# Page gathers of the sample's attention issued ahead, and the planner told of it

## Chip, cores and metric

The kernel runs on one core of a Trainium2 chip. The metric is the device time of one execution in microseconds (us). TensorE (PE) multiplies matrices, VectorE (DVE) and ScalarE (ACT) do elementwise work, GpSimd (POOL) does nothing here but issue indirect DMAs (gathers), and SyncE (SP) issues all the other DMAs. Each engine takes its own instructions strictly in order and waits on semaphores for the others.

## What is computed

One decoder layer is applied to a prompt of 1024 tokens and to a sample batch of 8 sequences of 4 new tokens, each sequence with 2048 cached tokens in pages of 128. After an input projection there are two mixers, a sparse attention and a retention; behind them stands a product-key expert layer (PEER) that gathers 128 expert rows for each token.

```python
# sparse attention of the sample batch
sc = indexer_scores(qi, wi, all_ik)          # all_ik: index keys by page, and the new ones
_, sel = lax.top_k(sc, 256)
k_sel = cache_k_l[phys, off]; v_sel = cache_v_l[phys, off]
att = sparse_attend(qa, k_sel, v_sel, valid)
...
# expert layer, for each token: 8 heads x 16 experts
hval = jnp.einsum('thkd,td->thk', u_emb[eid], xb)
coef = gate * gelu(hval)
y = jnp.einsum('thk,thkd->td', coef, v_emb[eid])
```

## The kernel before

Tokens are worked in nine tiles: tiles 0 to 7 are 128 prompt tokens each, tile 8 holds the 32 sample tokens. Each tile passes a front (attention and retention), a back (output projection, norm, choice of the experts) and its experts. The experts are the bulk. One slot is one expert of each of the tile's 128 tokens: an indirect DMA fetches 128 rows of 2048 floats (1.05 MB) into one of the 8 buffers of `ring`; VectorE forms the dot product of its first half with the tokens (L1476); ScalarE makes a 128x128 diagonal of coefficients from it; TensorE adds diagonal times second half to `yacc` (L1023). Two slots make a unit. In the order of work `unit` is the gather, the dot product and the diagonal, and `sums` the products on TensorE. There are 528 units in all, numbered 0 to 527 here: tile 6 has units 384 to 447. The gather of a slot waits until the slot eight before it has been summed (`row_used`), so at most four units are gathered ahead of `sums`.

A planner, `make_schedule`, writes one list of steps before the kernel is built, and every engine issues its part of each step in the order of that list. It keeps a clock for TensorE and one for VectorE, gives each step a cost and a lag (the time from its end to when the next step of its stream may start), and takes, among the steps that could start soonest, the one that is due first. So a lag in a table like `front_steps` decides how many units stand between two steps, on every engine.

The front of tile 8 computes the sample's attention beside the experts of tiles 5, 6 and 7:

- `sspread`, `swi`, `swiT` lay out the index weights; then nine steps `sscores`. Step b below 8 turns index-key page b on TensorE (L1094), ScalarE copies it, TensorE adds the weighted scores of page b-1 (L1102) and forms the dots of page b (L1108). Step 8 ends the sum. The sum goes by four small DMAs of SyncE to another place (`spare<-mid`), and `splace` (L1555) copies it together on VectorE.
- 32 steps `topk` on VectorE (MAX8 on L1338, MATCH_REPLACE8 on L1339) pick 256 of 2080 scores; `slogits` steps stand between them. Step (b, c) turns a quarter of key page b (L1135, bank `sKT`) and forms logits. After `mask`, the softmax and four steps `svalue` with the value pages; then key pages 4 to 7 and value pages 4 to 7 for the second half of the sequences.
- Beside them run the steps of the back of tile 7: `out` (L960, with chunks of `w_out` that SyncE loads two ahead), `add`, `norm`, `peerq`, `keys`, `top`.

The page gathers, 8 of index keys (0.52 MB each), 8 of keys and 8 of values (1.05 MB each), are issued by GpSimd between the expert gathers, from one place:

```python
pool.indirect_dma_start(dst, None, table, bass.IndirectOffsetOnAxis(ap=ids, axis=0)).then_inc(s, 16)
```

They land in two halves of `G` (the front of `kv`), in a part of `Hb`, and in a part of `spare`. Each is issued at the step that uses it, with a wait on the step that read the buffer before.

Of the kernel before, what the change touches and what calls it, by code (L numbers as in the profile page):

```python
# [24 lines left out]
P = 128  # L25
D = 1024
# [201 lines left out]
def front_steps(t):  # L228
# [27 lines left out]
    else:  # L256
        steps = [Step("load", t, 0, "", 0, 1, 12.0), Step("sheads", t, 0, "P", 3.0, 1, 2.5), Step("spad", t, 0, "D", 4.0, 2, 0.3),
                 Step("sdecay", t, 0, "P", 1.2, 2), Step("sdecayed", t, 0, "D", 4.5, 1, 0.3), Step("sret", t, 0, "P", 10.0, 1, 0.5)]
        for k in range(NB + 1):
            if k < NB:  # L260
                steps += [Step("skd", t, k, "D", 0.6, 0, 0.3), Step("sstate", t, k, "P", 1.7, 1, 0.4)]
            if k:
# [4 lines left out]
                  Step("swiT", t, 0, "D", 1.6, 1, 0.3)]  # L267
        steps += [Step("sscores", t, b, "P", 6.5, 1, 8.0 if b < NB else 1.2) for b in range(NB + 1)]
# [6 lines left out]
        for g in range(2):  # L275
            if g:
                steps += [Step("slogits", t, (b, c), "P", 2.0, 1, 1.2 if c < 5 else 4.0) for b in range(4, 8) for c in range(6)]
# [68 lines left out]
def make_schedule():  # L346
# [19 lines left out]
    def arrival(t, k):  # L366
        free = chosen[t] + LATENCY
# [104 lines left out]
def build(nc, x_p, x_s, cache_k, cache_v, cache_ik, state_in, pages, w_in, w_out, w_q, sk, uv,  # L472
# [15 lines left out]
    with ExitStack() as ctx:  # L488
# [66 lines left out]
        gathered = [G, Hb[:, 768:2816]]  # L555
        gathered_v = [G, spare[:, 2048:4096]]
# [120 lines left out]
        g_used = sem("g_used")  # L677
        smax_ready = sem("smax_ready")
# [137 lines left out]
        def _(pe):  # L816
# [268 lines left out]
            def sscores(t, b_):  # L1085


                if b_ < NB:
                    pe.wait_ge(g_in[b_ % 2], 16 * (b_ // 2 + 1))
                    for half in range(2):  # L1090
                        b = claim(("skT", b_, half))
                        for j in range(4):
                            c = 1024 * (b_ % 2) + (4 * half + j) * P
                            mm = nc.tensor.transpose(b[:, j * P:(j + 1) * P], G[:, c:c + P], ident)  # L1094
                        fill(mm, ("skT", b_, half))
# [29 lines left out]
            def slogits(t, part):  # L1125
# [3 lines left out]
                pe.wait_ge(g_in[bb % 2], 16 * (4 + 4 * g + bb // 2 + 1))  # L1129
# [42 lines left out]
            def svalue(t, part):  # L1172
# [4 lines left out]
                pe.wait_ge(g_in[bb % 2], 16 * (4 + 4 * g + 2 + bb // 2 + 1))  # L1177
# [639 lines left out]
        def _(pool):  # L1817
# [18 lines left out]

            def sscores(t, b):
                if b == NB:
                    return
                if b == 0:  # L1840
                    pool.wait_ge(gi_ready, 1)
                    pool.wait_ge(states_out, 16)
                if b >= 2:
                    filled(pool, ("skT", b - 2, 1))
                gather(G[:, 1024 * (b % 2):1024 * (b % 2 + 1)], table_ik, gi[:, b:b + 1], g_in[b % 2])

            def slogits(t, part):
# [78 lines left out]
```

## Time and profile before

| | us |
|---|---|
| median of 3 runs | 3803.05 (3802.86 to 3806.05) |
| the profiled execution, its own time | 3804.14 |
| its span in the trace | 3802.3 |
| VectorE busy in the span | 2595.7 |
| TensorE busy in the span | 3148.6 |

The span is the part of the execution that the trace shows; about 2 us lie around it. The page cuts it into 40 slices of 95 us, and gives busy shares in tenths; the DMA row there is the mean of the core's 16 DMA engines.

### The profile page before, as it was taken

Reading aid. Unit: us, or ns where it says so; the run is one execution under the profiler, and the core shown is the slowest. Engines: PE = TensorE matmul, PEld = TensorE weight load, DVE = VectorE, ACT = ScalarE, POOL = GpSimd, SP = SyncE. Lnnn points to the kernel's source line nnn. Section 1 sums busy time; section 2 is a strip of 40 time slices with the busy share of each in tenths; the row PEclk is TensorE's granted clock in tenths of the full one; section 3 lists DMA queues with packets and bytes.
Section 4 is the critical chain, followed back from the end, with each engine's and each line's share of the span. In section 5 each row is a group of like instructions: output and inputs, shape, how many; then the busy total and the mean of one; then the engine's idle time right before and its main releaser. Section 6 shows DMA issues by size and latency. Waiting matters only on the chain.

```text
span 3802.3 us, 31960 instructions
## 1 busy us (share of the span) xinstructions
PE 3148.6 (83%) x9551; PEld 1542.0 (41%) x9551; DVE 2595.7 (68%) x6051; ACT 1250.8 (33%) x3568; POOL 1240.7 (33%) x1084
## 2 busy tenths in 40 slices
PE   5999855898789879987987899789888288896877
PEld 2444344443244435433543454345433144342421
DVE  1222137877877878898889888998855998443645
ACT  1111122263235424532542264226333033331322
POOL 0000001444334434442443344334342034442432
PEclk9999977999999989998998999899999589998999
DMA  4111132999999999998999999899998179997998
GB/s 173 53 53 51 44 148 104 420 420 421 369 421 410 421 362 407 421 420 360 411 416 366 363 398 417 339 371 409 358 400 353 54 291 421 421 384 268 421 421 344
DMA packets 190430, 1245.76 MB, mean 328 GB/s; under 512 B 22704, under 2 KB 27184, under 8 KB 50672
## 3 DMA queue, kind: packets, MB, share of 16 engines
q0 software_dynamic: 155520, 1128.34, 72.8%
q1 hardware_dynamic: 34736, 115.37, 8.0%
q8 instruction: 77, 1.26, 0.1%
q14 instruction: 97, 0.79, 0.1%
HBM read 1220.50 MB, written 22.46 MB: 327 GB/s over the span
## 4 chain that ended last, share of the span: by engine, by line
PE 47%; DMA 25%; DVE 21%; issue 2%; ACT 2%; SPq 1%; POOL 1%; ACTq 0%; DVEq 0%; POOLq 0%
PE yacc L1023 24%; DMA weights<-in_uv,eid 20%; PE bank L850 11%; DVE weights L1476 6%; DVE kv L1339 4%; DVE tiny L1338 3%; PE bank L986 3%; PE bank L960 2%; DMA weights<-in_w_out 2%; DMA out_y_p<-nw 1%; PE bank L936 1%; PE bank L914 1%; DVE weights L1208 1%; POOL weights L1823 1%; SPq L715 1%
## 5 line engine op out<-in xcount | busy, mean ns | idle before, releaser
L1023 PE MATMUL yacc<-weights,diag 128*128 128x512 f32 (+1 forms) x4224 | 1961.0, 613 | 234.9 <-ACT diag L1743 234.3
L1823 POOL DMA_INDIRECT weights<-in_uv,eid x1056 | 1212.8, 1148 | 2503.5 <-PE yacc L1023 1797.1
L1476 DVE CUSTOM_DVE_ANT_0 weights<-weights,xn 128x1024 f32<-128x1024 f32 x1056 | 1274.8, 1225 | 598.0 <-DMA weights<-in_uv,eid 584.8
L1023 PEld LDWEIGHTS yacc<-weights,diag 128*128 128x128 f32 (+1 forms) x4224 | 791.4, 193 | 1295.4 <-issue 901.6
L1733 ACT ACTIVATE gl<-hv 128x2 f32<-128x2 f32 x528 | 107.1, 203 | 1522.2 <-DVE hv L1476 1521.2
L1743 ACT ACTIVATE diag<-main,coef 128x128 f32<-128x128 f32 x1024 | 359.0, 394 | 156.6 <-PE yacc L1023 140.7
L1736 ACT ACTIVATE coef<-gl,gate 128x1 f32<-128x1 f32 x1056 | 253.4, 287 | 17.3
L960 PE MATMUL bank<-weights 128*128 128x512 f32 (+1 forms) x288 | 160.9, 697 | 109.4 <-DMA weights<-in_w_out 107.6
L1338 DVE MAX8 tiny<-kv 128x8 f32<-128x384 f32 (+6 forms) x224 | 245.0, 1094 | 3.1
L1339 DVE MATCH_REPLACE8 kv<-tiny,kv 128x384 f32<-128x384 f32 (+6 forms) x224 | 241.6, 1079 | 0.0
L850 PE MATMUL bank<-weights 128*128 128x512 f32 (+3 forms) x560 | 230.1, 573 | 0.0
L850 PE MATMUL bank<-weights,mid 128*128 128x512 f32 (+1 forms) x448 | 183.2, 571 | 0.0
L850 PEld LDWEIGHTS bank<-weights 128*128 128x128 f32 (+1 forms) x560 | 97.6, 175 | 130.6 <-issue 125.8
L986 PEld LDWEIGHTS bank<-weights 128*128 128x128 f32 x1152 | 142.2, 203 | 17.6 <-issue 12.0
L986 PE MATMUL bank<-weights 128*128 128x128 f32 (+1 forms) x1152 | 143.1, 286 | 3.5 <-ACT weights L1695 3.5
L960 PEld LDWEIGHTS bank<-weights 128*128 128x128 f32 (+1 forms) x288 | 56.8, 206 | 199.2 <-issue 197.0
L1243 DVE TENSOR_TENSOR weights<-Hb,weights 128x80 f32<-128x80 f32 (+5 forms) x15 | 5.8, 387 | 191.1 <-ACT tinya L1624 190.8
L850 PEld LDWEIGHTS bank<-weights,mid 128*128 128x128 f32 x448 | 84.8, 190 | 96.7 <-issue 91.8
L1409 DVE FIND_INDEX8 weights<-weights 128x8 uint32<-128x128 f32 (+1 forms) x396 | 109.1, 288 | 0.0
L1243 DVE TENSOR_TENSOR weights<-spare,weights 128x80 f32<-128x80 f32 (+2 forms) x12 | 4.7, 389 | 142.2 <-ACT tinya L1624 141.9
L1405 DVE MAX8 weights<-weights 128x8 f32<-128x128 f32 (+1 forms) x396 | 96.1, 284 | 2.0 <-ACT weights L1719 0.8
L974 PE MATMUL bank<-main,xn 128*128 128x128 f32 (+1 forms) x72 | 13.8, 355 | 96.5 <-DVE xn L1392 96.5
(243 smaller groups left out, 2366.4 us busy)
## 6 DMA issues: line engine op xcount, KB each, us to landing
weights<-in_w_out SPq DMA_DIRECT2D x72, 512.0 KB, 7.8
weights<-in_uv,eid POOLq DMA_INDIRECT x1056, 11.6
Hb<-h_scratch SPq DMA_DIRECT2D x8, 1700.0 KB, 10.6
weights<-in_w_in SPq DMA_DIRECT2D x6, 2048.0 KB, 19.0
h_scratch<-Hb SPq DMA_DIRECT2D x4, 1700.0 KB, 5.5
h_scratch<-spare SPq DMA_DIRECT2D x4, 1700.0 KB, 5.5
nw<-in_wffn SPq DMA_DIRECT2D x9, 512.0 KB, 5.3
nw<-in_wfin SPq DMA_DIRECT2D x9, 512.0 KB, 14.0
```

The source lines that it names most:

```text
L850: mm = nc.tensor.matmul(b[0:R, 0:w], xT[t % 2][:, k, 0:R], win[:, k, 512 * n:512 * n + w], start=(k == 0), stop=(k == KC - 1))
L960: mm = nc.tensor.matmul(b[0:R, :], mixT[:, k, 0:R], wout_sb[i % 2][:, 512 * (k - k2):512 * (k - k2 + 1)], start=(k == 0), stop=(k == KC - 1))
L986: mm = nc.tensor.matmul(b[:, (h % 4) * R:(h % 4 + 1) * R], wq_sb[:, k, h * P:(h + 1) * P], nT[:, k, 0:R], start=(k == 0), stop=(k == KC - 1))
L1023: mm = nc.tensor.matmul(yacc[0:W, 512 * j:512 * (j + 1)], diag[:, n % 4, 0:W], ring[:, n % RING, D + 512 * j:D + 512 * (j + 1)], start=Fal ...
L1338: link(V.max(tiny[0:R, 40:48], a))
L1339: link(V.match_replace(a, tiny[0:R, 40:48], a, CHOSEN))
L1409: ins = V.max_index(idxs[:, half], vals[:, half], a)
L1476: ins = V.tensor_tensor_reduce(u, u, xn[:, t % 2, :], 1.0, 0.0, ALU.mult, ALU.add, hv[:, n % RING:n % RING + 1])
L1733: A.activation(gl[:, c:c + PAIR], hv[:, c:c + PAIR], ACT.Gelu).then_inc(gelu_ready, 1)
L1736: ins = A.activation(coef[:, c + s:c + s + 1], gl[:, c + s:c + s + 1], ACT.Copy, scale=gates[:, PAIR * k + s:PAIR * k + s + 1])
L1743: A.activation(diag[:, n % 4, 0:W], select[:, 0:W], ACT.Copy, scale=coef[:, n % RING:n % RING + 1]).then_inc(diag_ready, 1)
L1823: pool.indirect_dma_start(dst, None, table, bass.IndirectOffsetOnAxis(ap=ids, axis=0)).then_inc(s, 16)
```

## The change

The page gathers move forward in GpSimd's order, index keys get four buffers and semaphores of their own instead of two halves of `G`, and the planner is told shorter lags for the steps that used to wait for a page. One more rule in the planner's `arrival` forbids a unit ahead of the sums of the unit two before it.

```diff
-                  Step("swiT", t, 0, "D", 1.6, 1, 0.3)]
-        steps += [Step("sscores", t, b, "P", 6.5, 1, 8.0 if b < NB else 1.2) for b in range(NB + 1)]
+                  Step("swiT", t, 0, "D", 1.6, 1, 12.0)]
+        steps += [Step("sscores", t, b, "P", 6.5, 1, 2.0 if b < NB else 1.2) for b in range(NB + 1)]
...
-                steps += [Step("slogits", t, (b, c), "P", 2.0, 1, 1.2 if c < 5 else 4.0) for b in range(4, 8) for c in range(6)]
+                steps += [Step("slogits", t, (b, c), "P", 2.0, 1, 1.2) for b in range(4, 8) for c in range(6)]
...
     def arrival(t, k):
+        n0 = SLOTS * t + PAIR * k
+        if any(n >= 0 and n not in summed for n in range(n0 - 4, n0 - 4 + PAIR)):
+            return None
...
+        ik_pages = [Hb[:, 768:1792], Hb[:, 1792:2816], kv[:, 0:1024], kv[:, 1024:2048]]
...
+            def ik_page(b):
+                gather(ik_pages[b % 4], table_ik, gi[:, b:b + 1], ik_in[b % 4])
+
+            def k_page(b):
+                gather(gathered[b % 2], table_k, gi[:, b:b + 1], g_in[b % 2])
+
+            def v_page(g, bb):
+                gather(gathered_v[bb % 2], table_v, gi[:, 4 * g + bb:4 * g + bb + 1], g_in[bb % 2])
+
+            def swi(t, part):
+                pool.wait_ge(gi_ready, 1)
+                pool.wait_ge(gated, TILES + 1)
+                pool.wait_ge(wi_spread, 1)
+                ik_page(0)
+                ik_page(1)
+                pool.wait_ge(states_out, 16)
+                ik_page(2)
+                ik_page(3)
+
             def sscores(t, b):
-                if b == NB:
-                    return
-                if b == 0:
-                    pool.wait_ge(gi_ready, 1)
-                    pool.wait_ge(states_out, 16)
-                if b >= 2:
-                    filled(pool, ("skT", b - 2, 1))
-                gather(G[:, 1024 * (b % 2):1024 * (b % 2 + 1)], table_ik, gi[:, b:b + 1], g_in[b % 2])
+                if 1 <= b <= NB - 4:
+                    filled(pool, ("skT", b - 1, 1))
+                    ik_page(b + 3)
+                elif b == NB:
+                    filled(pool, ("skT", NB - 1, 1))
+                    k_page(0)
+                    k_page(1)
 
             def slogits(t, part):
                 b, c = part
-                if c:
+                if c != 4 or b % 4 == 3:
                     return
-                if b == 0:
-                    filled(pool, ("skT", NB - 1, 1))
-                elif b in (4, 5):
-                    pool.wait_ge(g_used, b - 1)
-                elif b % 4 >= 2:
-                    filled(pool, ("sKT", b - 2, 3))
-                gather(gathered[b % 2], table_k, gi[:, b:b + 1], g_in[b % 2])
+                filled(pool, ("sKT", b, 3))
+                if b % 4 < 2:
+                    k_page(b + 2)
+                else:
+                    v_page(b // 4, 0)
```

The waits of TensorE on the pages count on the new semaphores, and `svalue` and `sout` on GpSimd issue the value pages and key pages 4 and 5 in the same manner, each when the step that read its buffer is done.

What this does to the order of work is seen at three places. The line numbers of the changed kernel are 5 higher here; in these lists a unit on TensorE is four rows of `yacc` (the trace counts eight matmuls for them).

On TensorE, from the second product of `sscores` 6 to the end of the scores, the kernel before has two units and two `out` between two scores:

```order
L1102 MATMUL bank<-kv,spare 128x512
L1108 MATMUL bank<-mid,spare 32x512 x4
L960 MATMUL bank<-weights 128x512 x2
L1023 MATMUL yacc<-weights,diag 128x512 x4
L960 MATMUL bank<-weights 128x512 x2
L1023 MATMUL yacc<-weights,diag 128x512 x4
L1094 MATMUL bank<-main,kv 128x128 x8
L1102 MATMUL bank<-kv,spare 128x512
L1108 MATMUL bank<-mid,spare 32x512 x4
L960 MATMUL bank<-weights 128x512 x2
L1023 MATMUL yacc<-weights,diag 128x512 x8
L1102 MATMUL bank<-kv,spare 128x512
```

and the changed kernel one or none:

```order
L1107 MATMUL bank<-kv,spare 128x512
L1113 MATMUL bank<-mid,spare 32x512 x4
L1028 MATMUL yacc<-weights,diag 128x512 x4
L1099 MATMUL bank<-main,kv 128x128 x8
L1107 MATMUL bank<-kv,spare 128x512
L1113 MATMUL bank<-mid,spare 32x512 x4
L965 MATMUL bank<-weights 128x512 x2
L1107 MATMUL bank<-kv,spare 128x512
```

Here L1094 (now L1099) turns a page, L1102 (L1107) adds the scores, L1108 (L1113) is the dots, L960 (L965) is `out`, and the last row of both lists is the end of the sum. What moved is the units: 20 of them (377 to 396) stood between `swiT` and `splace`, now it is 11 (378 to 388).

On VectorE, the kernel before has 21 top-k steps, an `add` and a `norm` in one piece between unit 396 and unit 397. Around the `add` (`h<-bank`) it reads there:

```order
L1338 MAX tiny<-kv 32x8
L1339 MATCH_REPLACE kv<-tiny,kv 32x2080
L1384 TENSOR_TENSOR h<-bank,h 128x512
L1338 MAX tiny<-kv 32x8
L1339 MATCH_REPLACE kv<-tiny,kv 32x2080
L1338 MAX tiny<-kv 32x8
L1339 MATCH_REPLACE kv<-tiny,kv 32x2080
```

The changed kernel has 12 top-k steps between unit 388 and unit 389; this is the end of that piece (a unit is two pairs of ISA rows):

```order
L1343 MAX tiny<-kv 32x8
L1344 MATCH_REPLACE kv<-tiny,kv 32x2080
L1343 MAX tiny<-kv 32x8
L1344 MATCH_REPLACE kv<-tiny,kv 32x2080
L1389 TENSOR_TENSOR h<-bank,h 128x512
L1343 MAX tiny<-kv 32x8
L1344 MATCH_REPLACE kv<-tiny,kv 32x2080
L1481 ISA weights,hv<-weights,xn 128x1024
L1481 ISA hv 128x1
L1481 ISA weights,hv<-weights,xn 128x1024
L1481 ISA hv 128x1
L1343 MAX tiny<-kv 32x8
```

Behind it stands one unit after nearly every top-k step, to the same unit 406 ahead of `mask` in both kernels. So units 389 to 396 moved from ahead of the top-k into it.

On GpSimd, with the semaphores waited for, the kernel before from index page 7 to key page 3 (`full` counts a filled PSUM bank, here a turned page):

```order
L1823 DMA kv<-in_cache_ik,gi 128x1024 [waits full2]
L1823 DMA weights<-in_uv,eid 128x2048 [waits row_used] x6
L1823 DMA kv<-in_cache_k,gi 128x2048 [waits full0]
L1823 DMA Hb<-in_cache_k,gi 128x2048
L1823 DMA kv<-in_cache_k,gi 128x2048 [waits full1]
L1823 DMA weights<-in_uv,eid 128x2048 [waits row_used] x8
L1823 DMA Hb<-in_cache_k,gi 128x2048 [waits full2]
L1823 DMA weights<-in_uv,eid 128x2048 [waits row_used] x24
```

and the changed kernel from index page 7 on:

```order
L1828 DMA kv<-in_cache_ik,gi 128x1024 [waits full0]
L1828 DMA weights<-in_uv,eid 128x2048 [waits row_used] x4
L1828 DMA kv<-in_cache_k,gi 128x2048 [waits full0]
L1828 DMA Hb<-in_cache_k,gi 128x2048
L1828 DMA weights<-in_uv,eid 128x2048 [waits row_used] x2
L1828 DMA kv<-in_cache_k,gi 128x2048 [waits full1]
L1828 DMA weights<-in_uv,eid 128x2048 [waits row_used] x4
L1828 DMA Hb<-in_cache_k,gi 128x2048 [waits full2]
L1828 DMA weights<-in_uv,eid 128x2048 [waits row_used] x16
L1828 DMA kv<-in_cache_v,gi 128x2048 [waits full3]
```

Key pages 0 and 1 now stand ahead of the last unit before the top-k, and key page 3 stands behind four expert gathers instead of eight, ahead of sixteen.

## Rows read from the trace of the kernel before

**Rows 1.** Of the page: DMA share in tenths and GB/s in 40 slices
```profile
DMA  4111132999999999998999999899998179997998
GB/s 173 53 53 51 44 148 104 420 420 421 369 421 410 421 362 407 421 420 360 411 416 366 363 398 417 339 371 409 358 400 353 54 291 421 421 384 268 421 421 344
```

**Rows 2.** Busy us of PE, PEld, DVE, ACT, POOL by stretch; clock, DMA share, GB/s
```profile
2779.10:2906.40 127.30, 108.31 (x334) 47.27 (x333) 56.05 (x101) 42.79 (x128) 49.71 (x45) 0.95 1.01 406
2906.40:3021.10 114.70, 32.86 (x117) 15.43 (x116) 106.78 (x91) 16.12 (x32) 9.39 (x10) 0.63 0.27 106
3021.10:3100.10 79.00, 69.45 (x250) 37.51 (x249) 78.17 (x79) 22.52 (x67) 23.13 (x20) 0.90 0.68 252
3100.10:3425.20 325.10, 288.28 (x888) 134.46 (x886) 198.32 (x491) 114.58 (x344) 141.53 (x125) 0.96 0.97 399
3425.20:3509.90 84.70, 55.61 (x145) 22.03 (x144) 25.81 (x55) 12.45 (x47) 20.58 (x17) 0.80 0.68 249
3509.90:3753.10 243.20, 195.17 (x502) 77.75 (x501) 137.00 (x280) 69.60 (x248) 101.53 (x95) 0.97 1.01 421
```

**Rows 3.** VectorE in order of time (start us, length us), 2902 to 3100
```profile
2905.27 1.22 DVE L1476 CUSTOM_DVE_ANT_0 weights<-weights,xn 128x1024 f32<-128x1024 f32 x1 [1.22 <-DMA weights<-in_uv,eid]
...
2912.36 1.90 DVE L1555 COPY kv<-spare 32x512 f32<-32x512 f32 x4 [5.76 <-DMA spare<-mid]
...
2914.51 2.32 DVE L1338 MAX8 tiny<-kv 32x8 f32<-32x2080 f32 x1
...
2919.26 2.32 DVE L1338 MAX8 tiny<-kv 32x8 f32<-32x2080 f32 x1
...
3021.13 1.23 DVE L1476 CUSTOM_DVE_ANT_0 weights<-weights,xn 128x1024 f32<-128x1024 f32 x1
...
3022.28 1.22 DVE L1476 CUSTOM_DVE_ANT_0 weights<-weights,xn 128x1024 f32<-128x1024 f32 x1
...
3096.45 1.23 DVE L1349 TENSOR_SCALAR kv<-kv 32x2080 f32<-32x2080 f32 x1
```

**Rows 4.** GpSimd in order of time, 2896 to 3030
```profile
2898.94 0.94 POOL L1823 DMA_INDIRECT kv<-in_cache_k,gi  x1 [0.30 <-issue]
...
2933.63 0.94 POOL L1823 DMA_INDIRECT Hb<-in_cache_k,gi  x1 [0.30 <-issue]
3028.20 0.94 POOL L1823 DMA_INDIRECT weights<-in_uv,eid  x1 [93.64 <-PE yacc L1023]
```

**Rows 5.** VectorE in order of time, 2790 to 2796
```profile
2794.05 1.23 DVE L1476 CUSTOM_DVE_ANT_0 weights<-weights,xn 128x1024 f32<-128x1024 f32 x1 [1.26 <-DMA weights<-in_uv,eid]
```

**Rows 6.** TensorE in order of time, 2784 to 2804
```profile
2800.45 1.04 PE L1094 MATMUL bank<-main,kv 128*128 128x128 f32 x8
...
2802.27 1.06 PE L1108 MATMUL bank<-mid,spare 128*32 128x512 f32 x8
```

**Rows 7.** TensorE in order of time, 2840 to 2860
```profile
2852.34 1.88 PE L960 MATMUL bank<-weights 128*128 128x512 f32 x4
...
2854.06 3.60 PE L1023 MATMUL yacc<-weights,diag 128*128 128x512 f32 x8
```

**Rows 8.** TensorE in order of time, 2898 to 2912
```profile
2899.70 1.02 PE L1102 MATMUL bank<-kv,spare 128*128 128x512 f32 x2
```

**Rows 9.** Of the page: DMA issues, median us from issue to landing
```profile
weights<-in_w_out SPq DMA_DIRECT2D x72, 512.0 KB, 7.8
```

**Rows 10.** Gathers from the index-key table
```profile
DMA to landing us min/median/max: 10.9/13.8/14.9
```

**Rows 11.** Gathers from the key table
```profile
DMA to landing us min/median/max: 5.7/12.8/18.0
```

**Rows 12.** GpSimd in order of time, 3228 to 3240
```profile
3230.36 0.94 POOL L1823 DMA_INDIRECT weights<-in_uv,eid  x1 [2.39 <-PE yacc L1023]
3232.07 0.97 POOL L1823 DMA_INDIRECT weights<-in_uv,eid  x1 [0.78 <-PE yacc L1023]
```

**Rows 13.** TensorE in order of time, 3228 to 3240
```profile
3231.64 0.60 PE L1135 MATMUL bank<-main,Hb 128*128 128x128 f32 x4
```

More of the change, by code:

```diff
@@ L677, in build @@
         g_used = sem("g_used")
+        ik_in = [sem(f"ik_in{i}") for i in range(4)]
         smax_ready = sem("smax_ready")
@@ L1088, in sscores @@
                 if b_ < NB:
-                    pe.wait_ge(g_in[b_ % 2], 16 * (b_ // 2 + 1))
+                    pe.wait_ge(ik_in[b_ % 4], 16 * (b_ // 4 + 1))
                     for half in range(2):
@@ L1092, in sscores @@
                         for j in range(4):
-                            c = 1024 * (b_ % 2) + (4 * half + j) * P
-                            mm = nc.tensor.transpose(b[:, j * P:(j + 1) * P], G[:, c:c + P], ident)
+                            c = (4 * half + j) * P
+                            mm = nc.tensor.transpose(b[:, j * P:(j + 1) * P], ik_pages[b_ % 4][:, c:c + P], ident)
                         fill(mm, ("skT", b_, half))
@@ L1128, in slogits @@
                 g, bb = b_ // 4, b_ % 4
-                pe.wait_ge(g_in[bb % 2], 16 * (4 + 4 * g + bb // 2 + 1))
+                pe.wait_ge(g_in[bb % 2], 16 * (4 * g + bb // 2 + 1))
                 Gk = gathered[b_ % 2]
@@ L1176, in svalue @@
                 o = bank(("satt", g)) if bb else claim(("satt", g))
-                pe.wait_ge(g_in[bb % 2], 16 * (4 + 4 * g + 2 + bb // 2 + 1))
+                pe.wait_ge(g_in[bb % 2], 16 * (4 * g + 2 + bb // 2 + 1))
                 ob = o[32 * bb:32 * bb + 32, 0:P]
@@ L1861, in svalue, with sout @@
                 if bb == 0:
-                    filled(pool, ("sKT", 4 * g + 2, 3))
-                elif bb == 1:
                     filled(pool, ("spT", g, 4))
-                else:
-                    pool.wait_ge(g_used, 4 * g + bb - 1)
-                gather(gathered_v[bb % 2], table_v, gi[:, 4 * g + bb:4 * g + bb + 1], g_in[bb % 2])
-            steps = {"unit": unit, "sscores": sscores, "slogits": slogits, "svalue": svalue}
+                    v_page(g, 1)
+                elif bb < 3:
+                    pool.wait_ge(g_used, 4 * g + bb)
+                    v_page(g, bb + 1)
+                elif g == 0:
+                    pool.wait_ge(g_used, 3)
+                    k_page(4)
+            def sout(t, g):
+                if g == 0:
+                    pool.wait_ge(g_used, 4)
+                    k_page(5)
+            steps = {"unit": unit, "swi": swi, "sscores": sscores, "slogits": slogits, "svalue": svalue, "sout": sout}
             for what, t, part in schedule:
```

## The prediction

> **What bounds the kernel now.** I read the page's slices first. From slice 8 on the DMA engines are busy nine tenths or more in most slices, at up to 421 GB/s, and slice 32 stands out with 54 GB/s [rows 1]. So the kernel is bound by its gathers nearly everywhere, and what matters is where the DMA engines idle. I then cut the time around the sample's attention into stretches [rows 2]. The steady one, 3509.9 to 3753.1, shows the floor: 421 GB/s. A unit is two gathers of 128 x 2048 x 4 bytes, 2.10 MB, so 4.98 us. In 2779.1 to 2906.4 (units 377 to 396 with seven index pages) the DMA share is 1.01. In 2906.4 to 3021.1 it is 0.27, and VectorE is busy 106.8 of 114.7 us. In 3021.1 to 3100.1 it is 0.68, VectorE 78.2 of 79.0. Then the DMA engines bound again (0.97), but for a gap of the tail of tile 8 (0.68 of 84.7 us).
>
> The timeline of VectorE says what the hole is: its last dot product, of unit 396, begins at 2905.3; the scores arrive at 2912.4 after 5.8 us of waiting, the top-k begins at 2914.5, and unit 397 starts only at 3021.1 [rows 3]. The ring of eight buffers is full, and GpSimd waits 93.6 us for a buffer [rows 4]. From 2914.5 to the end of `mask` at 3097.7 VectorE does not pause: it alone sets the pace there. The hole is 21 top-k steps of 4.75 us (2914.51 to 2919.26), an `add` and a `norm` in one piece.
>
> The waits of TensorE on index pages, which the change attacks by name, cost nothing in themselves: they fall where the DMA share is 1.01.
>
> **The change, part by part.** *Where the burst of scores begins.* In the old order, VectorE is done with unit 379 at 2795.3 [rows 5]. In the new one all four first index pages go out ahead of unit 378, where one did; three more pages of 0.52 MB stand ahead of unit 379, 3.7 us at 421 GB/s. Its diagonals (about 1.4 us, an estimate from ScalarE's place between dot and product) and sums (3.6 us [rows 7]) then end at 2795.3 + 3.7 + 1.4 + 3.6 = 2804.0. `sscores` 0 starts there. At that point the pages are 20 us old, more than the 14.9 us that the slowest took [rows 10].
>
> *The burst.* A scores step takes 2.9 us on TensorE when its page is there (2800.45 to 2803.33) [rows 6], a unit 3.6, an `out` 1.9 [rows 7]; the seed of tile 6 has as many matmuls as an `out`. Steps 0 to 3 with four units: 4 x 2.9 + 4 x 3.6 + 0.7 (step 0 has no product to cover its copies, my choice) = 26.7. Then step 4, seed, step 5, unit, step 6, unit, step 7, `out`, and the sum's end of 1.0 [rows 8]: 4 x 2.9 + 2 x 1.9 + 2 x 3.6 + 1.0 = 23.6. For ScalarE, whose copies stand behind the diagonals of a unit, I add 2. That is 52.3 us, to 2856.3. The DMA engines need less: six units and four pages are 35 us. Pages 4 to 7 go out three steps (some 19 us) ahead.
>
> *From the sum to the top-k.* Before: 2900.7 to 2914.5, 13.8 us [rows 8, 3]. The same work stands there now, so the top-k begins at 2870.1, against 2914.5. Unit 388 goes ahead of it; its gathers stand behind key pages 0 and 1, which wait for page 7 to be turned (about 2850), and 2 x 2.5 + 5.0 us of transfer and the issues bring it in before 2870.
>
> *The top-k run.* VectorE's work from there to the end of `mask` was 183.2 us with ten units. It now holds 18: eight more at 2 x 1.15 us [rows 3] are 18.4. That gives 201.6, to 3071.7.
>
> *A new wait in it.* On TensorE `slogits` (1, 3) stands behind four `out`. The third needs PSUM bank 5, which the `add` after top-k step 10 frees (2870.1 + 52.3 + 0.7 = 2923.1), and the later ones need `w_out` chunks, 7.8 us each from issue to landing [rows 9]. So the turned quarter of key page 1 comes at 2936 to 2941; on GpSimd key page 3 waits for it, and behind page 3 the gathers of unit 391, which VectorE wants at 2942. No row shows that wait. Below it is nothing; above, the last gather is issued at about 2944 and takes 11.6 us as in the busy stretches, 12 late. The DMA engines are idle there and the fastest key page took 5.7 us [rows 11]; nearer to that row I take 4. So `mask` ends at 3075.7, against 3097.7: **22.0 us earlier**, with the same 407 units behind it.
>
> By the Trainium skill (DMA: Bandwidth & Descriptors, Anatomy of one DMA) a gather costs about 2.0 us and its bytes over 436 GB/s, 3.2 us for an index page and 4.4 for a key page, wherever it stands. The trace shows 10.9 to 14.9 and 5.7 to 18.0 [rows 10, 11], since a page queues behind up to eight expert gathers. By the skill's figure the new wait would be near 0 and the sum 26 us; by the trace's median it would be some 10 and the sum 16.
>
> *Behind it.* From 3100 to 3425 the same bytes flow at a DMA share of 0.97, so the shift is carried, neither grown nor lost. Here GpSimd waits for a turned quarter that stands one step ahead, with row gathers queued behind. The trace has that place: page 5's quarter is turned at 3232.2 [rows 13], and the gathers which would stand behind it went out at 3230.4 and 3232.1 [rows 12]. They would be 3 us later, with two units (10 us of transfer) still in flight: cost nothing. `mixT` of tile 8 comes four units earlier but with as many units between it and `sout` (three), so the gap of the tail stays. The new rule in `arrival` shifts single units by one place between units 284 and 375; the bytes are the same and the DMA engines mostly full: 0, with 3 us either way.
>
> The profiled execution took 3804.14 us; 3804.1 - 22.0 = 3782.1. The median of the runs is 1.1 lower, so **3781 us**. A measurement tells 0.2%, 8 us, from no change.
>
> **Rivals.** (a) *The forecast*, top-k earlier by 44 us and given back by 22. Its own range: without the new wait, ScalarE's 2 and the late start, 32 us, 3771; with 12 for the wait and 5 more ahead of the top-k, 9 us, 3794. Chance 0.62.
>
> (b) *More than that.* The tail's gap (0.68 of 84.7 us is 27 us idle) [rows 2] also shrinks because its steps fall otherwise among the units, and value pages come earlier. For it: four `out` of tile 8 stand with fewer units ahead. Against it: TensorE waits there for small DMAs and `w_out`, which are not changed. Half of 27 on top of 26 (no new wait): 3764. Chance 0.12.
>
> (c) *No change.* The burst does not run at TensorE's pace. Each page adds a wait on GpSimd with two row gathers behind it, and the scores' four DMAs stand on SyncE behind the store of tile 5's output and a `w_out` chunk. If the top-k began at 2892, 22 us later than I hold, all would be given back: 3803. For it: eight steps in 52 us have no row like it, and pages did take 14.9 us. Against it: pages are three steps ahead. Chance 0.12.
>
> (d) *Slower.* Head-of-line waits on GpSimd in the stretch that the DMA engines bound. Of key pages 4 to 7 and the value pages, ten wait for something done a step or two earlier with gathers queued behind; if each emptied the DMA queues for longer than 2.2 us, the gain would be gone, and at most each costs one unit, 4.98: 3781 + 50 = 3831; at 3.5 us each, 3816. Against it: the margin at 3232 above. Chance 0.10.
>
> (e) *The planner's lags do not reach the engines.* The order lists exclude it; 0.04 is left for things not seen, half of it on either side.
>
> **How the numbers follow.** Faster by over 0.2% (below 3795): (a), (b) and half of (e), less 0.02 for (a)'s edge: 0.74. Slower: (d) with half of (e) and a part of (c): 0.13. Same: 0.13. The range takes in (a), (b) and the near half of (c): 3763 to 3801.
>
> **What would show it.** In the changed profile: the first MAX8 of 2080 scores at 2870 with the dot product of unit 388 ahead of it, 12 top-k steps up to unit 389, `mask` ending at 3076; eight scores steps on TensorE within 55 us; a wait of VectorE for a gather of unit 391; DMA share 0.97 or more from `mask` to unit 464. The prediction is wrong if the top-k begins after 2885, if VectorE waits for gathers for more than 12 us within the run, or if units after `mask` take more than 5.7 us each (325.1 us for 57 before).

## The result and the profile after

The changed kernel took 3788.19 us (median of 5, 3783.29 to 3790.74) against 3803.05 before (median of 5 with the runs taken beside it, 3801.44 to 3809.26). The ratio is 0.9952, 95% interval 0.9940 to 0.9964: 0.5% faster. Forecast were 3781 us and a range of 3763 to 3801. The profiled execution of the changed kernel took 3783.29 us, 20.9 less than that of before (3804.14). It is the fastest of the five, so the trace shows more of a gain than the 14.9 us between the medians.

The page of the changed kernel, its DMA share and GB/s in 40 slices, answers to [rows 1]:

```profile
DMA  4111142999999999999999899989994779997998
GB/s 174 53 53 49 45 150 97 419 421 421 364 420 412 417 366 403 416 415 375 397 421 396 336 389 421 365 360 399 387 370 180 296 290 408 421 391 292 421 421 345
```

The hole of two slices (54 and 291 GB/s) has become three shallower ones (180, 296, 290), and the slice at tile 8's tail shows 292 where it showed 268. The same stretches as in [rows 2], by the windows view of the changed kernel (busy us of PE, PEld, DVE, ACT, POOL; clock, DMA share, GB/s):

```profile
2776.60:2875.75 99.15, 79.86 (x277) 35.14 (x277) 38.21 (x78) 33.01 (x93) 29.09 (x29) 0.95 0.88 347
2875.75:2933.50 57.75, 20.31 (x59) 8.29 (x58) 56.93 (x37) 7.54 (x14) 4.68 (x5) 0.65 0.26 100
2933.50:3083.00 149.50, 113.91 (x369) 55.49 (x367) 142.44 (x154) 40.60 (x120) 46.07 (x42) 0.92 0.77 296
3083.00:3400.00 317.00, 274.95 (x858) 128.34 (x858) 194.82 (x486) 110.08 (x329) 131.97 (x118) 0.95 0.97 395
3400.00:3490.60 90.60, 69.22 (x174) 28.07 (x175) 31.78 (x63) 16.57 (x62) 24.52 (x23) 0.85 0.75 284
3490.60:3732.50 241.90, 192.26 (x503) 77.53 (x501) 136.97 (x280) 69.61 (x248) 103.88 (x97) 0.99 1.01 421
```

The stretch in which VectorE works alone and the DMA engines stand at 0.26 is 57.75 us long, where 114.7 were [rows 2]; the one in which units run among the top-k steps is 149.5 us, where 79 were. VectorE of the changed kernel in order of time, from the end of the scores:

```profile
2868.38 1.23 DVE L1481 CUSTOM_DVE_ANT_0 weights<-weights,xn 128x1024 f32<-128x1024 f32 x1 [20.07 <-DMA weights<-in_uv,eid]
...
2872.24 1.23 DVE L1481 CUSTOM_DVE_ANT_0 weights<-weights,xn 128x1024 f32<-128x1024 f32 x1 [2.62 <-DMA weights<-in_uv,eid]
...
2873.60 1.90 DVE L1560 COPY kv<-spare 32x512 f32<-32x512 f32 x4
...
2875.75 2.32 DVE L1343 MAX8 tiny<-kv 32x8 f32<-32x2080 f32 x1
...
2951.50 1.23 DVE L1481 CUSTOM_DVE_ANT_0 weights<-weights,xn 128x1024 f32<-128x1024 f32 x1 [3.81 <-DMA weights<-in_uv,eid]
...
2953.91 1.22 DVE L1481 CUSTOM_DVE_ANT_0 weights<-weights,xn 128x1024 f32<-128x1024 f32 x1 [1.17 <-DMA weights<-in_uv,eid]
...
3081.77 1.23 DVE L1354 TENSOR_SCALAR kv<-kv 32x2080 f32<-32x2080 f32 x1
```

Unit 388 comes 20.07 us late, the scores that wait behind it are copied without a wait, and the top-k begins at 2875.75, not at 2914.51 [rows 3]. Unit 391 is waited for 3.81 + 1.17 = 5.0 us. `mask` ends at 3083.0, 14.7 us before the 3097.7 of the old order. GpSimd's rows say why both units were late, and the first of them shows one more such wait, ahead of the scores:

```profile
2771.99 0.94 POOL L1828 DMA_INDIRECT Hb<-in_cache_ik,gi  x1 [6.76 <-DVE spare L1543]
...
2855.26 0.93 POOL L1828 DMA_INDIRECT kv<-in_cache_k,gi  x1 [18.79 <-PE bank L1099]
2856.49 0.93 POOL L1828 DMA_INDIRECT Hb<-in_cache_k,gi  x1 [0.30 <-issue]
2857.73 0.94 POOL L1828 DMA_INDIRECT weights<-in_uv,eid  x1 [0.30 <-issue]
...
2941.78 0.93 POOL L1828 DMA_INDIRECT Hb<-in_cache_k,gi  x1 [49.42 <-PE bank L1140]
2943.02 0.93 POOL L1828 DMA_INDIRECT weights<-in_uv,eid  x1 [0.30 <-issue]
```

Index page 0 waits 6.76 us for the spread index weights, with three more pages and the gathers of the units after 377 behind it. Key pages 0 and 1 wait 18.79 us for the last turned index page, with unit 388's gathers behind; key page 3 waits for its turned quarter, with unit 391's behind. And TensorE of the changed kernel: the first scores step, its three waits for ScalarE within the eight steps, the sum's last product, the `out` that waited for the `add`, and the turned quarter:

```profile
2804.08 1.04 PE L1099 MATMUL bank<-main,Hb 128*128 128x128 f32 x8
2806.06 1.06 PE L1113 MATMUL bank<-mid,spare 128*32 128x512 f32 x8 [0.94 <-ACT mid L1776]
...
2815.82 1.06 PE L1113 MATMUL bank<-mid,spare 128*32 128x512 f32 x8 [3.33 <-ACT mid L1776]
...
2838.41 1.06 PE L1113 MATMUL bank<-mid,spare 128*32 128x512 f32 x8 [1.74 <-ACT mid L1776]
...
2858.59 1.02 PE L1107 MATMUL bank<-kv,spare 128*128 128x512 f32 x2
...
2928.93 5.76 PE L965 MATMUL bank<-weights 128*128 128x512 f32 x8 [36.88 <-DVE h L1389]
...
2940.91 0.60 PE L1140 MATMUL bank<-main,Hb 128*128 128x128 f32 x4
```

### The profile page after: what moved, and what is told of

It reads as the page before. It is cut to its first block, busy times and chain, and to the rows that moved or that the text cites. A ratio compares the mean times of both kernels' runs of the same rounds, so it can differ in the third digit from the quotient of the medians.

```text
span 3781.5 us, 31964 instructions
## 1 busy us (share of the span) xinstructions
PE 3142.6 (83%) x9551; PEld 1535.3 (41%) x9551; DVE 2594.0 (69%) x6051; ACT 1249.5 (33%) x3568; POOL 1233.8 (33%) x1084
## 4 chain that ended last, share of the span: by engine, by line
PE 47%; DMA 25%; DVE 21%; ACT 3%; issue 2%; SPq 1%; POOL 1%; ACTq 0%; DVEq 0%; POOLq 0%
PE yacc L1028 24%; DMA weights<-in_uv,eid 20%; PE bank L855 11%; DVE weights L1481 7%; DVE kv L1344 3%; DVE tiny L1343 3%; PE bank L991 3%; PE bank L965 2%; DMA weights<-in_w_out 2%; PE bank L941 1%; PE bank L919 1%; DVE weights L1213 1%; DMA out_y_p<-nw 1%; POOL weights L1828 1%; SPq L720 1%
## 5 line engine op out<-in xcount | busy, mean ns | idle before, releaser
L965 PE MATMUL bank<-weights 128*128 128x512 f32 (+1 forms) x288 | 158.3, 687 | 144.5 <-DMA weights<-in_w_out 106.4
L965 PEld LDWEIGHTS bank<-weights 128*128 128x128 f32 (+1 forms) x288 | 56.5, 205 | 232.9 <-issue 231.2
L919 PEld LDWEIGHTS bank<-kv,mid 128*128 128x128 f32 x576 | 75.9, 198 | 33.6 <-issue 22.8
## 6 DMA issues: line engine op xcount, KB each, us to landing
weights<-in_uv,eid POOLq DMA_INDIRECT x1056, 11.5
```

What stands on the lines that cost most here:

```text
L919: mm = nc.tensor.matmul(o[:, g * HD:(g + 1) * HD], mid[:, m % 2, k * P:(k + 1) * P], vall[:, kt, HD * (g % 2):HD * (g % 2) + HD], start=(k ...
L965: mm = nc.tensor.matmul(b[0:R, :], mixT[:, k, 0:R], wout_sb[i % 2][:, 512 * (k - k2):512 * (k - k2 + 1)], start=(k == 0), stop=(k == KC - 1))
```

## Experiments

Two theories at the start. **The order**: the gain is that the planner's lags move eight units from ahead of the top-k into it; the gathers ahead have no part in it. **The pages**: the gain is that pages are there when TensorE wants them. A third, that the new rule in `arrival` does it. The profiles are compared from the end of unit 376 (its second dot product) to the end of unit 527, the last: at unit 376 the profiled executions already lay between 2772.3 and 2782.0 us, although no experiment is about the code ahead of it. "From unit 376" below means such a difference. By it the changed kernel's `mask` ends 12.2 us earlier than before (306.4 against 318.6), not 14.7: the other 2.5 us were already there at unit 376.

**Old lags, gathers ahead and rule kept.**

```diff
-                  Step("swiT", t, 0, "D", 1.6, 1, 12.0)]
-        steps += [Step("sscores", t, b, "P", 6.5, 1, 2.0 if b < NB else 1.2) for b in range(NB + 1)]
+                  Step("swiT", t, 0, "D", 1.6, 1, 0.3)]
+        steps += [Step("sscores", t, b, "P", 6.5, 1, 8.0 if b < NB else 1.2) for b in range(NB + 1)]
```

(and 4.0 again for the last `slogits` of a block)

> The changed kernel with the three lags of before (swiT 0.3, sscores 8.0, last slogits of a block 4.0): gathers issued ahead and the new planner rule stay. Theory (the gain is the order: eight units moved from ahead of the sample's top-k into it): the top-k stands behind unit 397 again, begins at about 2915, mask ends near 3098, and the time is 3803 within 4 us, ratio 1.000. Rival (pages fetched ahead are what saves time): the scores steps no longer wait for pages and the time stays near that of the changed kernel, 3788, ratio 0.996.

Measured: 3799.44 us (median of 12), ratio 0.9982 (0.9974 to 0.9991). `mask` ends at 3098.6 and the time is within 4 us of 3803, as the theory of the order has it; the rival's 3788 is excluded. One thing differs from what I expected: the top-k begins at 2924.5, 10 us later than before, since the rule alone also moves steps there (the third experiment).

**New lags and rule, the old gathers** (before's code for GpSimd and its two index-key buffers).

> The kernel before with the new lags and the planner's new rule, but its own gathers (two index-key buffers, each page issued at its own step). Same order of VectorE and TensorE as in the changed kernel. Theory: most of the gain is here already, since the eight units move. The eight scores steps, each of whose pages is issued only two steps ahead and takes 11 to 15 us to land, need 60 us or so in place of 55 (5 us lost), but key pages 0 and 1 are issued behind unit 388's gathers, so VectorE does not wait 20 us for that unit (5.6 us won): 3788, 3782 to 3796, ratio 0.996. Rival (pages ahead are needed): the index pages come so late that the burst takes 75 us or more, and the gain is gone: 3803 or above.

Measured: 3778.59 us (median of 6), ratio 0.9932 (0.9916 to 0.9947): faster than the whole change, and than both theory and rival allowed. So the gathers ahead are not the gain but a cost. (The interval overlaps that of the changed kernel's first set, 0.9940 to 0.9964, a little, and not that of the second set below; from unit 376 to unit 527 the profiled executions take 982.9 us here, 990.9 and 989.5 there.) In this kernel's VectorE rows unit 388 comes early and the top-k waits for the scores' way through DRAM instead, and unit 391 (2946.72) is not waited for:

```profile
2855.52 1.23 DVE L1479 CUSTOM_DVE_ANT_0 weights<-weights,xn 128x1024 f32<-128x1024 f32 x1 [4.34 <-DMA weights<-in_uv,eid]
...
2872.63 1.91 DVE L1558 COPY kv<-spare 32x512 f32<-32x512 f32 x4 [11.47 <-DMA spare<-mid]
...
2946.72 1.23 DVE L1479 CUSTOM_DVE_ANT_0 weights<-weights,xn 128x1024 f32<-128x1024 f32 x1
```

I had expected the scores steps to take 5 us more with pages issued only two steps ahead, 60 in place of 55. They take 59.1 (2800.7 to 2859.8), 3.6 more than the changed kernel's 55.5, and one page is waited for:

```profile
2813.47 1.97 PE L1097 MATMUL bank<-main,kv 128*128 128x128 f32 x8 [5.45 <-DMA kv<-in_cache_ik,gi]
```

But they begin 21.1 us after unit 376, where the changed kernel, with four index pages and their 6.76 us wait ahead of the next units' gathers, needs 27.4. What pages ahead save within the scores they cost at their start, and the sum ends 80.2 us after unit 376 here and 83.0 there.

**The rule alone on the kernel before** (three lines of `arrival`, no lag, no gather changed).

> The kernel before with the planner's new rule alone (a unit is not planned before the pair of rows four ahead of it is summed). It moves one unit later and mixT of tile 8 behind unit 466 in place of 464. Theory: no change within 3 us, 3803, ratio 1.000. Rival (the rule is what saves): 3790. With the old-lags kernel it gives the price of the gathers ahead under the old order: theory 0 within 3 us, since no VectorE or DMA time is in it.

Measured: 3797.66 us (median of 12), ratio 0.9981 (0.9970 to 0.9991). My "no change within 3 us" was wrong: the rule is worth some 7 us by the ratio, and 12.5 from unit 376 in the profiled executions. Beside the first experiment it shows that gathers ahead give nothing under the old lags (0.9982 and 0.9981; in the profiled executions they cost 7.1 us). The 12.5 us lie in two places. Behind `mask` are 7.7 of them: VectorE's waits by the waits view, units 449 to 456, first the kernel before (3327.2 to 3379.7), then this one (3325.3 to 3369.1):

```profile
DVE weights L1476 <- DMA weights<-in_uv,eid: 23.0, 10, 7.7
```

```profile
DVE weights L1479 <- DMA weights<-in_uv,eid: 16.8, 11, 3.7
```

The kernel before waits 7.7 us for unit 456, whose buffers come free with the sums of unit 452, and these are planned behind unit 454 and a value step. The rule keeps a unit behind the sums of the unit two before it, and they stand ahead of unit 453.

Ahead of `mask` are the other 4.8. Under the rule unit 397, the `add` and the `norm` stand ahead of the top-k, in part in the time in which VectorE waited 5.76 us for the scores [rows 3]:

```profile
2907.60 0.68 DVE L1387 TENSOR_TENSOR h<-bank,h 128x512 f32<-128x512 f32 x1
...
2919.12 1.91 DVE L1558 COPY kv<-spare 32x512 f32<-32x512 f32 x4 [2.36 <-DMA spare<-mid]
```

The top-k begins 4.4 us later from unit 376 and ends 4.8 us earlier, since 9.1 us of work are gone from it. With the gathers ahead it begins another 5.3 us later, and these 4.8 us are lost. So beside the kernel with the rule the new lags move nine units, 389 to 397, not eight.

**All top-k rounds spread** (on the changed kernel, with key pages 0, 1 and 3 issued later as in the next two).

```diff
-            steps += [Step("topk", t, k, "D", 4.8, 0, 0.3)]
+            steps += [Step("topk", t, k, "D", 4.8, 1, 4.0)]
```

> The changed kernel with the sample's 32 top-k rounds spread: each made ready 4 us after the one before in the planner, so that one or two units stand behind each round (the mask behind unit 432 in place of 406), and key pages 0, 1 and 3 issued later. Theory (in the top-k VectorE is the bound and the DMA queues are idle: 0.26 busy in the first 58 us of it, 0.77 in the next 150): the idle queues are filled, about 50 to 85 us of DMA idle is to be had less what the tail of tile 8 takes back (its mixT moves 24 units later, to unit 484, and its experts must be chosen before its own first unit at 512): 3735, 3715 to 3760, ratio 0.985. Rival (the end of the kernel is set by tile 8's own chain from its scores to its experts, not by the sum of DMA work): the tail grows by what the hole gives, 3788 to 3810.

Measured: 3780.43 us (median of 6), ratio 0.9932 (0.9914 to 0.9950). Neither number: unit 408 ends at 2990.8, 117 us earlier than before, and 27 are left at the end of the profiled execution. Three stretches of its windows view show who takes them back:

```profile
2877.00:3020.00 143.00, 129.08 (x411) 64.01 (x412) 137.73 (x196) 46.86 (x146) 55.56 (x50) 0.94 0.97 395
3020.00:3179.00 159.00, 107.16 (x219) 42.53 (x218) 155.09 (x303) 40.16 (x121) 43.79 (x43) 0.84 0.74 286
...
3490.00:3625.00 135.00, 106.24 (x320) 54.57 (x320) 56.82 (x150) 26.77 (x92) 33.72 (x32) 0.81 0.70 269
```

At first both VectorE and the DMA engines are full (0.97). Then VectorE, at 155.1 of 159 us, also has tile 7's expert choice in its way. In tile 8's tail, which now comes 24 units later, the planner puts that tile's steps in one piece (because it takes them as overdue, as I read its code; no run tests that); TensorE's rows show four query projections between two units' sums, 24 us in which no buffer comes free:

```profile
3554.86 9.99 PE L991 MATMUL bank<-weights 128*128 128x32 f32 x64
3565.30 13.84 PE L991 MATMUL bank<-weights 128*128 128x32 f32 x64 [0.46 <-ACT weights L1700]
```

**Key pages 0 and 1 behind unit 388** (on the changed kernel).

```diff
-                elif b == NB:
-                    filled(pool, ("skT", NB - 1, 1))
-                    k_page(0)
-                    k_page(1)
...
+            def splace(t, part):
+                filled(pool, ("skT", NB - 1, 1))
+                k_page(0)
+                k_page(1)
```

> The changed kernel with key pages 0 and 1 issued at splace, behind unit 388's gathers, in place of ahead of them. Theory from the traces (unit 388 and the spread scores now land within a few us of each other, so freeing one leaves the other): unit 388 comes in near 2860, the first top-k waits for the scores' spread instead and begins at 2873 to 2877; no change against the changed kernel within 3 us, 3788, ratio 0.995. Rival (unit 388 alone set the start): the top-k begins at 2870, 5.6 us earlier, 3782.

Measured: 3784.44 us (median of 5), ratio 0.9937 (0.9924 to 0.9951). Its VectorE rows: unit 388 is there at 2859.4, and the copy of the scores waits until 2872.2:

```profile
2859.38 1.23 DVE L1481 CUSTOM_DVE_ANT_0 weights<-weights,xn 128x1024 f32<-128x1024 f32 x1 [8.28 <-DMA weights<-in_uv,eid]
...
2872.24 1.91 DVE L1560 COPY kv<-spare 32x512 f32<-32x512 f32 x4 [6.00 <-DMA spare<-mid]
...
2874.40 2.31 DVE L1343 MAX8 tiny<-kv 32x8 f32<-32x2080 f32 x1
```

The top-k begins 1.4 us earlier than with the change, and counted from unit 376 by 3 to 4 us: after 94.9 us, where the two profiled executions of the changed kernel need 99.1 and 98.0, and the next experiment, whose order is the same up to there, 96.4. Of the 20 us for which unit 388 was waited, 1.5 to 4.2 thus count at the top-k, and 0.4 to 1.8 at unit 527 (989.1 against 990.9 and 989.5). The medians say more, 3.8 to 9 us less than the changed kernel's two, and lie between my theory and the rival; the traces do not show where that comes from.

**Key page 3 four units later** (on the changed kernel).

```diff
+                if part == (2, 0):
+                    filled(pool, ("sKT", 1, 3))
+                    k_page(3)
-                if c != 4 or b % 4 == 3:
+                if c != 4 or b % 4 == 3 or b == 1:
                     return
```

> The changed kernel with key page 3 issued four units later on GpSimd (at slogits (2,0), behind unit 393's gathers) so that nothing stands ahead of unit 391's gathers behind the bank that waits for the add. Theory (the 6 us between the changed kernel and the one with the new lags and the old gathers arise at unit 391 alone, 2955.1 against 2949.1): VectorE's wait of 3.8 + 1.2 us there goes, mask ends at 3077 in place of 3083, and the time falls by 6: 3782, ratio 0.9935. Rival (the rest of the early gathers holds units up too, in the DMA-bound stretch): less than 2 us come back, 3787.

Measured: 3783.59 us (median of 5), ratio 0.9941 (0.9927 to 0.9955); in the trace unit 391 is not waited for, `mask` ends at 3078.0, and units 376 to 527 take 984.4 us against 990.9. The 5.0 us of the wait are there; 1.5 us to the kernel with the old gathers (982.9) are left. The medians can't tell this experiment from the last one (3784.44), although unit 391 is still waited for there; that the wait is gone is shown by the trace alone.

**One unit behind nearly each round** (on new lags with old gathers; as the spread above with 2.0 for 4.0).

> The kernel with the new lags and the old gathers, and each of the 32 top-k rounds made ready 2 us after the one before, so that one unit stands behind nearly each round: the mask stands behind unit 415 in place of 406, mixT of tile 8 behind 464 in place of 460. Theory (the top-k is VectorE-bound: a unit adds 2.6 us of VectorE time to it and takes 5.0 us of DMA time out of what follows): nine units more, 2.4 us each, 22 us less than the same kernel without it: 3757, 3750 to 3768, ratio 0.988. Rival (tile 8's chain, which ends later by four units, gives it back as the wide spread showed): 3778, no change against that kernel.

Measured: 3771.26 us (median of 5), ratio 0.9897 (0.9880 to 0.9914), 7 us less by the medians than without the spread and 13 by the ratios (0.9932 to 0.9897), not 22. From the top-k's start to the end of `mask` it needs 230.2 us where that kernel needs 202.2: 28.0 more. Nine units at 2.3 are 20.7 of it; the other 7.3 are about the three steps of tile 7's expert choice, which used to lie among DMA-bound units and cost nothing there. Its rows by the lines view, of that stretch (the kernel without the spread has none of them there):

```profile
L1412 DVE FIND_INDEX8 weights<-weights 128x8 uint32<-128x128 f32 x12 | 3.3, 285 | 0.0
L1408 DVE MAX8 weights<-weights 128x8 f32<-128x128 f32 x12 | 2.9, 283 | 0.1
L1410 DVE MATCH_REPLACE8 weights<-weights 128x128 f32<-128x128 f32 x6 | 1.6, 275 | 0.0
```

Behind `mask` it gains 35.8 us (table below) for nine units fewer, not 9 x 4.98 = 44.8. So 7.9 of the 22 arrive in the profiled executions.

**More units ahead of tile 8's mixT** (on new lags with old gathers).

```diff
-            steps += [Step("sout", t, g, "D", 0.8, 1, 14.0 if g else 0.3)]
+            steps += [Step("sout", t, g, "D", 0.8, 1, 30.0 if g else 0.3)]
```

> The kernel with the new lags and the old gathers, and 30 us in place of 14 planned between the sample's second sout and mixT of tile 8, so that three more units (463 in place of 460) stand ahead of mixT. Theory (TensorE waits 15.6 us for the sample's attention output to come back from DRAM with the sums behind it, and the DMA queues run dry): the wait is covered by the three units, 10 to 15 us less than the same kernel without it: 3766, ratio 0.990. Rival (what empties the queues is the wait for w_out's pages and the add, 25 us, which stays): within 3 us of it, 3778.

Measured: 3772.42 us (median of 4), ratio 0.9907 (0.9892 to 0.9922), 6 us less by the medians, between theory and rival, and 3.6 from unit 376. TensorE's wait for the attention output is 5.28 us, where the same kernel without the longer lag had 16.45 and the changed kernel 15.64; the waits for `w_out` behind it stay (13.2 us in two, 12.9 without the longer lag):

```profile
3406.28 1.03 PE L952 MATMUL bank<-main,Hb 32*128 32x32 f32 x8 [5.28 <-DMA Hb<-a_scratch]
```

**Three kernels beside each other**: the changed kernel again; both gains together (topk lag 2.0, sout lag 30.0); and the same with the first rounds spread wider, by

```diff
+            steps += [Step("topk", t, k, "D", 4.8, 1, 4.0 if k < 12 else 2)]
```

> The changed kernel itself once more, so that it shares the runs of the kernel before with the two beside it. Its runs so far lay near 3783.5 and near 3790.7; both theories give 3783 to 3791, ratio 0.995.

> New lags, old gathers, one unit behind nearly each top-k round, and 30 us planned between the last sout and mixT of tile 8. Theory (the two gains arise in two places, the top-k and tile 8's tail, about 6 us each over the kernel with the new lags and old gathers): they add, 3766, 3760 to 3772, ratio 0.9895. Rival (tile 8's chain ends last, and each alone only used up the same slack): 3772, as each alone.

> As the one beside it, but with up to two units behind each of the first twelve top-k rounds, so that the mask stands behind unit 421 in place of 415. Theory (the first half of the top-k has idle DMA queues, 0.89 and 0.76 busy with one unit a round, and VectorE time goes there anyway): six more units by 2.4 us, less some 5 us for the steps of tile 7's experts that now lie in the VectorE-bound stretch: 3757 to 3764, ratio 0.988. Rival (the later tile 8's chain ends, the more of its waits lie bare): 3766 or above, nothing over the one beside it.

Measured: the changed kernel 3793.39 us (median of 6, 3783.08 to 3795.71), ratio 0.9966 (0.9953 to 0.9978); both gains 3758.15 us (median of 4), 0.9874 (0.9860 to 0.9889); spread wider 3747.35 us (median of 5), 0.9847 (0.9835 to 0.9860). The changed kernel again lies above the 3783 to 3791 that I expected. Both gains together and the wider spread lie below their theories (3760 to 3772 and 3757 to 3764), and both rivals are excluded. The last beats both kernels of this study by far. Its windows view from the top-k's start to the end of `mask` shows how long the DMA engines stay busy there now:

```profile
2861.70:2950.00 88.30, 78.63 (x243) 37.76 (x242) 82.89 (x107) 25.35 (x82) 33.60 (x30) 0.96 0.97 388
2950.00:3020.00 70.00, 56.96 (x194) 29.30 (x194) 66.73 (x83) 22.30 (x66) 24.86 (x23) 0.93 0.88 358
3020.00:3120.50 100.50, 55.51 (x119) 21.76 (x117) 99.33 (x159) 22.94 (x63) 21.71 (x21) 0.76 0.55 203
```

All kernels side by side: the median, and from the profiled executions the differences of the ends of unit 376, of `mask` and of unit 527, in us. (The runs of the kernel before had medians of 3803.1 to 3806.2 in the four sets, so the ratios above compare more exactly than the medians here.)

| kernel | median | unit 376 to mask | mask to 527 | unit 376 to 527 |
|---|---|---|---|---|
| before | 3803.05 | 318.6 | 690.6 | 1009.2 |
| rule only | 3797.66 | 313.8 | 682.9 | 996.7 |
| old lags, gathers ahead | 3799.44 | 319.2 | 684.6 | 1003.8 |
| changed | 3788.19 | 306.4 | 684.5 | 990.9 |
| changed, again | 3793.39 | 304.5 | 685.0 | 989.5 |
| key pages 0 and 1 later | 3784.44 | 301.7 | 687.4 | 989.1 |
| key page 3 later | 3783.59 | 298.6 | 685.8 | 984.4 |
| all rounds spread | 3780.43 | 402.4 | 582.5 | 984.9 |
| new lags, old gathers | 3778.59 | 297.4 | 685.5 | 982.9 |
| the same, sout lag 30 | 3772.42 | 297.2 | 682.1 | 979.3 |
| the same, topk lag 2 | 3771.26 | 325.3 | 649.7 | 975.0 |
| both | 3758.15 | 324.5 | 645.5 | 970.0 |
| both, wider | 3747.35 | 348.1 | 612.4 | 960.5 |

Behind `mask` come 121 units in most of them, 112 in the two with topk lag 2, 106 in the last, 95 with all rounds spread. In the last column the two gains add: 3.6 + 7.9 = 11.5 expected, 12.9 measured; the medians, of different sets, give 6.2 + 7.3 = 13.5 expected and 20.4 measured, but the ratios, which compare within a set, 0.25% + 0.35% = 0.60% expected and 0.58% measured.

## Why the prediction was right

The forecast's side and main mechanism held: the top-k began earlier with fewer units ahead of it, and the units that moved into it cost their VectorE time. Its size, 22.0 us, was reached by the profiled execution (20.9) and not by the medians (14.9, and 12.0 in the second set). Several terms were too small, all to the same side, and were made up in part by a term put at 0 and by luck.

**Start of the burst**: 2804.0 forecast, 2804.1 measured. This is luck. The changed kernel's execution was already 2.5 us ahead of the other at unit 376; from there, the forecast gives 24.9 us and the measurement 27.4. The dot product of unit 379 ends 21.4 us after unit 376, where it did after 16.2: 5.2 later, not the 3.7 of three pages' transfer. The sum has no term for the 6.76 us that GpSimd waits for the index weights with unit gathers behind.

**The burst**: 52.3 us forecast, 55.5 measured (2804.1 to 2859.6). The mis-sized term is the 2 us added for ScalarE: TensorE waited 0.94 + 3.33 + 1.74 = 6.0 us for it. No page was waited for in the eight steps.

**Sum to top-k**: 13.8 us forecast, 16.2 measured. I held that unit 388's gathers would be in before 2870. They were in at 2872, since the last page was turned at 2855, not at about 2850. With key pages 0 and 1 out of the way the scores set the start, 1.5 to 4.2 us earlier from unit 376: two things end close together, and removing one frees little.

**VectorE's run**: 201.6 us forecast without the wait. The kernels without the wait need 202.2 for the same 18 units (new lags with old gathers; key page 3 later). Right to 0.6.

**The new wait**: 4 us forecast, 5.0 measured, at the unit and by the chain named (`add`, `out`, turned quarter, key page 3, unit 391), and moving that page took it away. The gather issued at 2943.02 was used at 2951.50, 8.5 us later, nearer to the fastest key page's 5.7 [rows 11] than to the median of 12.8. By the Trainium skill (DMA: Bandwidth & Descriptors, Anatomy of one DMA) a gather of that size is estimated at 4.4 us, about 2.0 us and its bytes over 436 GB/s. These 8.5 us, in the idle stretch and behind one key page, lie between that and the 11.6 of the median row gather before. Together, by the clock of the execution: 3.3 + 2.4 + 0.6 + 1.0 = 7.3, and `mask` ended at 3083.0 in place of 3075.7. From unit 376 the late start of the burst is added: of the 22.0 us forecast at `mask`, 12.2 were measured (14.1 in the second profiled execution).

**"The shift is carried"** from `mask` on, with GpSimd's waits at "cost nothing": wrong over 200 us. GpSimd's waits in the changed kernel, 3083 to 3275:

```profile
POOL weights L1828 <- PE yacc L1028: 60.3, 33, 10.4
POOL Hb L1828 <- PE bank L1185: 12.6, 1, 12.6
...
POOL kv L1828 <- PE bank L1140: 9.5, 2, 5.4
POOL spare L1828 <- PE bank L1174: 4.3, 1, 4.3
POOL Hb L1828 <- PE bank L1140: 3.2, 1, 3.2
POOL kv L1828 <- PE bank L1185: 2.7, 2, 2.1
POOL spare L1828 <- PE bank L1185: 2.4, 1, 2.4
```

Before, pages waited there for nothing but their own issue. The pages' waits are 34.7 us. Most of them only took the place of waits for a unit's buffer, which are 60.3 us here and 96.0 before (3097.7 to 3285). They cost 5: units 407 to 440 end 192.4 us after `mask`, 187.2 before, 187.4 with the old gathers. That is rival (d) at about a tenth of its price. I had looked at one place (page 5's quarter) and taken it for all ten. The two other experiments with gathers ahead and new lags show the same (193.6 and 194.6), so this price is no accident of one execution. Part of it came back later.

**"The planner's rule: 0, 3 us either way"** and **"the gap of the tail stays"**: wrong, and to the good side. From unit 448 to 476 the kernel before takes 203.75 us; the changed one takes 196.12, 7.6 less, and the ten profiled executions with the rule whose tail of tile 8 lies in that stretch take 192.7 to 199.6. Under the old lags the rule alone gives 8.0 (203.8 to 195.8). Under the new lags it can't be told apart from rival (b)'s cause, that `out` steps fall otherwise among the units: the new lags without the rule were not tried. So the whole, in the profiled executions: -2.5 at unit 376, within the drift between executions (last section), -12.2 from there to `mask`, +2.6 to unit 448, -7.6 to 476, -1.1 behind, -20.8 against 22.0 forecast. Without the drift it is -18.3 (-19.7 in the second execution). The sum was right partly by errors that cancel. The rule's 4.8 us ahead of `mask`, which the forecast did not have either, are not seen apart here, since the new lags move the same steps again.

**The signs named beforehand**: the top-k began at 2875.75, later than 2870 and before the 2885 that would have refuted the forecast; 12 top-k steps up to unit 389 and the wait for unit 391 are there; the eight steps took 55.5 us, a little over the 55 named; the 57 units behind `mask` took 324.3 us, 5.7 each, and the DMA share was 0.95 in their first 192 us, below the 0.97 named.

**By parts, from the medians' ratios**: rule -0.19%; lags -0.49% more (0.9981 to 0.9932); gathers ahead +0.20 to +0.34% (0.9932 to 0.9952 and 0.9966). The part of the change that its name speaks of costs 8 to 13 us (6.6 to 8.0 from unit 376 in the profiled executions). 5 of them are the wait for unit 391. The rest lies in part with the waits on GpSimd behind `mask`, but the kernel without unit 391's wait is within 1.5 us of the old gathers in the profiled executions and 5 us above in the medians, so its size stays open; the two medians come from different sets, and by ratios (0.9941 and 0.9932) their intervals overlap. Also open is why most executions of the changed kernel that were not profiled took 3788 to 3796, while both profiled ones took 3783 to 3784.

## What to carry to other kernels

Where one engine is the bound of a stretch and the DMA engines of the rest, put into that stretch as much DMA-fed work as it can take: a unit cost 2.3 us of VectorE's time there and took 4.0 us off what followed (35.8 us for nine units; its transfer is 5.0), and it pays until the steps displaced come bare elsewhere. Prefetches issued on a queue in program order hold up everything behind them for as long as their buffer is not free; issue one only where its buffer has long been read. A wait that ends shortly after its neighbour is worth little, 1.5 to 4.2 us of 20 here, so look for the next release before you price it.

## What was not expected of the hardware

In the twelve profiled executions with the planner's rule VectorE has the same instructions in the same order up to unit 376, and yet that unit ended between 2772.3 and 2782.0 us, 0.35% apart; the two executions of the changed kernel itself ended it at 2776.6 and 2778.7: for effects of a few us, times counted from a place ahead of which nothing of interest differs (here unit 376) told more than spans. From there to unit 527 the same two took 990.9 and 989.5 us.
